# Attention buffers in another order, the cache loaded during layer 0's last expert, and five streams prepared ahead of the tokens' rows

## What is computed

```python
h = h + gmlp_mixer(rms_norm(h, norm_mix[0]), ...)
h = h + hier_moe(rms_norm(h, norm_ffn[0]), ...)          # 16 experts, 2 for each token
c = rms_norm(h, kv_norm) @ w_dkv                         # latent (256) and rotary key (32)
c_kv, k_rope = rms_norm(c[..., :256], ...), rope(rms_norm(c[..., 256:], ...), pos)
ckv_all = concatenate([past_ckv, c_kv]); krope_all = concatenate([past_krope, k_rope])
k_nope = rms_norm(einsum('blr,rhd->blhd', ckv_all, w_uk), k_nope_norm)   # per head
v = einsum('blr,rhd->blhd', ckv_all, w_uv)
q = low_rank_queries(rms_norm(h, norm_mix[1]))           # w_dq, norm, w_uq, norms, rope
o = softmax(masked(q_nope @ k_nope + q_rope @ k_rope) * SCALE) @ v
h = h + o @ w_o
h = h + hier_moe(rms_norm(h, norm_ffn[1]), ...)
```

## Time and profile before

| | |
|---|---|
| median of 3 runs | 1081.33 us |
| lowest and highest | 1079.39 and 1082.06 us |
| span of the profiled execution | 1080.6 us |
| granted clock of TensorE, mean over the span | 0.969 |
| PE busy (matmuls), DVE, ACT, POOL | 94%, 70%, 56%, 8% of the span |
| DMA | 278.95 MB, 258 GB/s in the mean |

### The profile page before, as it was taken

The page is one execution under the profiler, slowest core; times in us unless marked ns, Lnnn a source line. Parts: engine busy times, 40 slices in busy tenths (PEclk is TensorE's granted clock), DMA queues, the critical chain, the costliest instruction groups (busy, mean ns, idle before and its releaser), DMA issues.

```text
span 1080.6 us, 13540 instructions
## 1 busy us (share of the span) xinstructions
PE 1018.8 (94%) x5133; PEld 758.1 (70%) x5133; DVE 760.0 (70%) x645; ACT 605.0 (56%) x507; POOL 82.3 (8%) x109
## 2 busy tenths in 40 slices
PE   4999999999999999999969998989997989998997
PEld 4889998887666666666648686877785667766664
DVE  4456656267699888888815556662766999989896
ACT  5337432244577777777524233443536868887881
POOL 4000000004000000000021020000030000000003
PEclk9999999999999999999979999897898999999999
DMA  9542523684899999999366010303668999999984
GB/s 344 164 166 87 217 78 125 249 346 159 297 389 380 396 382 407 385 405 379 129 232 194 0 42 22 135 1 126 264 239 300 387 394 380 392 402 405 409 345 175
DMA packets 56923, 278.95 MB, mean 258 GB/s; under 512 B 6336, under 2 KB 10848, under 8 KB 48288
## 3 DMA queue, kind: packets, MB, share of 16 engines
q1 hardware_dynamic: 45424, 240.21, 57.7%
q0 software_dynamic: 8992, 29.74, 8.1%
q10 hardware_dynamic: 2464, 8.39, 2.0%
HBM read 260.45 MB, written 18.04 MB: 258 GB/s over the span
## 4 chain that ended last, share of the span: by engine, by line
PE 63%; issue 16%; DVE 8%; DMA 7%; ACT 3%; POOL 1%; ACTq 0%; SPq 0%; POOLq 0%; DVEq 0%
PE ps L189 19%; PE ps L195 9%; PE ps L527 4%; PE ps L581 4%; DMA raw<-in_moe_w_dram 4%; PE ps L624 3%; PE ps L1367 3%; PE ps L1364 3%; PE ps L2120 3%; PE ps L587 2%; PE ps L535 2%; DVE moe_wl L1104 2%; DVE raw_lo L1104 2%; PE ps L631 2%; PE ps L2095 1%
## 5 line engine op out<-in xcount | busy, mean ns | idle before, releaser
L1104 DVE TENSOR_TENSOR raw_lo<-raw,moe_wh 128x4096 fp32r<-128x4096 f32 x48 | 212.0, 4422 | 37.4 <-ACT moe_wh L1099 37.4
L1104 DVE TENSOR_TENSOR moe_wl<-moe_raw,moe_wh 128x4096 fp32r<-128x4096 f32 x48 | 212.0, 4422 | 33.6 <-ACT moe_wh L1099 33.4
L1099 ACT ACTIVATE moe_wh<-raw 128x4096 fp32r<-128x4096 f32 x48 | 174.0, 3625 | 20.8 <-DMA raw<-in_moe_w_dram 9.0
L1099 ACT ACTIVATE moe_wh<-moe_raw 128x4096 fp32r<-128x4096 f32 x48 | 173.9, 3624 | 14.1 <-DMA moe_raw<-in_moe_w_dram 14.1
L189 PE MATMUL ps<-moe_wh,moe_x 128*72 128x512 f32 x512 | 125.8, 398 | 1.7 <-DVE moe_x L1234 1.5
L189 PEld LDWEIGHTS ps<-moe_wh,moe_x 128*72 128x72 f32 x512 | 71.8, 143 | 46.0 <-DVE moe_x L1234 2.6
L329 DVE TENSOR_TENSOR raw_lo<-raw,gm_wh 128x4096 fp32r<-128x4096 f32 x12 | 53.1, 4424 | 69.6 <-ACT gm_wh L323 67.2
L189 PE MATMUL ps<-moe_wh,moe_hTh 128*72 128x512 f32 (+1 forms) x256 | 83.7, 410 | 4.9 <-DVE moe_hTl L1239 3.1
L189 PE MATMUL ps<-moe_wh,moe_hTl 128*72 128x512 f32 (+1 forms) x256 | 81.8, 401 | 0.0
L323 ACT ACTIVATE gm_wh<-raw 128x4096 fp32r<-128x4096 f32 x11 | 39.9, 3626 | 57.7 <-DMA raw<-in_gm_w_out_dram 29.2
L1364 PE MATMUL ps<-moe_wh,moe_x 128*128 128x512 f32 x224 | 58.9, 402 | 9.7 <-DVE moe_x L1234 9.7
(11 more groups left out here) (408 smaller groups left out, 1730.1 us busy)
## 6 DMA issues: line engine op xcount, KB each, us to landing
raw<-in_moe_w_dram SPq DMA_DIRECT2D x48, 2048.0 KB, 11.6
moe_raw<-in_moe_w_dram SPq DMA_DIRECT2D x48, 2048.0 KB, 11.9
raw<-in_gm_w_in_dram SPq DMA_DIRECT2D x7, 2048.0 KB, 7.9
raw<-in_gm_w_out_dram SPq DMA_DIRECT2D x4, 2048.0 KB, 7.6
moe_yrows<-moe_rows ACTq DMA_DIRECT2D x16, 288.0 KB
moe_rows<-moe_xrows POOLq DMA_DIRECT2D x14, 288.0 KB, 9.4
moe_rows<-moe_xrows POOLq DMA_DIRECT2D x14, 256.0 KB, 9.1
moe_yrows<-moe_rows ACTq DMA_DIRECT2D x14, 256.0 KB
```

The source lines that it names most:

```text
L1099: nc.scalar.activation(w_hi[hi][:], w_raw[slot], ACT.Copy).then_inc(wh_ready, 1)
L1104: nc.vector.tensor_tensor(w_lo[slot], w_raw[slot], w_hi[hi][:].bitcast(F32), ALU.subtract).then_inc(wl_ready, 1)
```

## The change

Four things are altered.

1. The attention's buffers are allocated in another order: `cTs`, `krT`, `psT`, `new_rinv`, `cTn` and `cqT` come first, on `moe_wh0` and `moe_wh1`, and `cst` and `w_uk` come to lie on the low parts of the weights 3 and 4, which are free at `w_used` = 45.
2. SP loads `w_uk` one product earlier (`3 * NE - 3`), and directly behind it both halves of the cache, before the overflow loop. `load_cache` is gone, and so is the second half's load in `at_sync`.
3. `turn_keys_up` stands before `product_y(15)` on TensorE, and `copy_keys_up` before `y_copy(15)` on ACT.
4. TensorE prepares stream 4 too before the rows, and then waits for `ch_c` 13 and `ch_sq` 10, since the rows' turns write the banks that ACT reads for that stream. Behind the projections come `prepare(5)` and `prepare(6)`, then `key_products(7)` between the first low-rank turn and the first query product; `turn_latent(0)` and `keys_and_values(0)` each come one place earlier. ACT's queue is reordered alike.

```diff
--- before.py
+++ after.py
@@ -833,8 +833,6 @@
                                      w_in_expert(l, name, e)).then_inc(s["w"], 16)
                     at_least(sp, s["act"], 5 * i + 5)
                     sp.dma_start(yrows[bass.ds(row, cap), :], rows[0:cap, 2, :]).then_inc(s["st"], 16)
-            if l == 0:
-                load_cache(sp)
             at_least(sp, s["st"], 16 * n_over + 16)
             sp.wait_ge(y_stored, 16 * (E0 + SENT if l else NE))
             sp.sem_inc(y_final, 1)
@@ -1205,10 +1203,10 @@
             experts(a, folding_step if l else step)
             if not l:
                 hidden_high(NE - 1)
+                copy_keys_up(a)
             y_copy(NE - 1, 1)
             if not l:
                 store_y(NE - 1, 1)
-                copy_keys_up(a)
             a.wait_ge(rt_table, l + 1)
             n_over = a.value_load(ovt_i[0:1, 2 * EXTRA:2 * EXTRA + 1], min_val=0, max_val=EXTRA)
             s = over[l]
@@ -1466,6 +1464,7 @@
             experts(pe, folding_step if l else step, {3: lambda: turn_kept(0)} if l else None)
             if not l:
                 transpose_hidden(NE - 1)
+                turn_keys_up(pe)
             if l:
                 pe.wait_ge(rt_hot, 4 + 1 + KEPT)
                 pe.wait_ge(y_out, E0 + NE - 1)
@@ -1483,8 +1482,6 @@
                         last = nc.tensor.matmul(ps[:, SPREAD[t][c]], kept_hot[0:cap, 1, t * P:(t + 1) * P].bitcast(F32),
                                                 rows[0:cap, 3, c * 512:c * 512 + 512], start=False, stop=True)
                     last.then_inc(spread, 1)
-            else:
-                turn_keys_up(pe)
             pe.wait_ge(rt_table, l + 1)
             n_over = pe.value_load(ovt_i[0:1, 2 * EXTRA:2 * EXTRA + 1], min_val=0, max_val=EXTRA)
             s = over[l]
@@ -1528,12 +1525,15 @@
         KC = 2 * P
         KALL = KC + DECS
         UNITS = [(0, 0, HEADS), (1, 0, HEADS // 2), (1, HEADS // 2, HEADS)]
+        cTs = sb("at_cache_cT", [P, DECB, 2, KC], F32, at)
+        krT = sb("at_krT", [QK, DECB + 1, KC], F32, at)
+        psT = sb("at_psT", [P, 2, 4 * P], F32, at)
+        new_rinv = sb("at_new_rinv", [P, P], F32, at)
+        cTn = sb("at_cTn", [P, 2, P], F32, at)
+        cqT = sb("at_cqT", [P, 3, P], F32, at)
         cst = sb("at_cache", [P, 2 * DECB, KVR + ROPE], F32, at)
-        cTs = sb("at_cache_cT", [P, DECB, 2, KC], F32, at)
         w_uk = sb("at_w_uk", [P, 2, HEADS * NOPE], F32, at)
-        krT = sb("at_krT", [QK, DECB + 1, KC], F32, at)
         rinv = sb("at_rinv", [P, DECB, KC], F32, at)
-        psT = sb("at_psT", [P, 2, 4 * P], F32, at)
         qa = sb("at_qa", [P, 2, DECB, HEADS * DECS], F32, at)
         sqT = qa[:].rearrange("p s b n -> p s (b n)")
         pcT = sb("at_pcT", [P, 2, HEADS, DECB, DECS], F32, at)
@@ -1552,7 +1552,6 @@
         ast = sb("at_stat", [P, 64], F32, at)
         qT = sb("at_qT", [QK, 2, HEADS, P], F32, at)
         qTs = gain2[0:QK].rearrange("p (b n) -> p b n", b=DECB)
-        cqT = sb("at_cqT", [P, 3, P], F32, at)
         turns = sb("at_turns", [P, 4, TILES, ROPE // 2], F32, at)
         kst = sb("at_kstat", [P, 2, HEADS], F32, at)
         kcat = sb("at_kcat", [P, 2, HEADS, QK], F32, at)
@@ -1560,8 +1559,6 @@
 
         kTp = raw[0:QK, 1, 0:HEADS * SEQ].rearrange("p (h k) -> p h k", h=HEADS)
         vp = raw[:, 1, HEADS * SEQ:HEADS * SEQ + 2 * HEADS * VD].rearrange("p (t n) -> p t n", t=2)
-        new_rinv = sb("at_new_rinv", [P, P], F32, at)
-        cTn = sb("at_cTn", [P, 2, P], F32, at)
         q_words = q_sb[:].rearrange("p t h n -> p (t h n)")
         s_sb = q_words[:, 0:DECB * KALL].rearrange("p (b k) -> p b k", b=DECB)
         sst = sb("at_sample_stat", [P, DECB, 3], F32, at)
@@ -1622,18 +1619,15 @@
                          ).then_inc(ld_cache[half], 16)
 
         def load_keys_up(sp):
-            sp.wait_ge(w_used, M_MOE[0] + 3 * NE - 2)
+            sp.wait_ge(w_used, M_MOE[0] + 3 * NE - 3)
             sp.dma_start(w_uk[:], A["w_uk"].rearrange("(k p) h n -> p k (h n)", p=P)).then_inc(ld_uk, 16)
-
-        def load_cache(sp):
-            sp.wait_ge(w_used, M_MOE[0] + 3 * NE - 1)
             load_cached(sp, 0)
+            load_cached(sp, 1)
 
         def at_sync(sp):
             sp.wait_ge(w_used, M_MOE[0] + 3 * NE)
             sp.dma_start(w_dkv, A["w_dkv"].rearrange("(k p) n -> p k n", p=P)).then_inc(ld_at, 16)
             sp.dma_start(w_dq, A["w_dq"][0].rearrange("(k p) n -> p k n", p=P)).then_inc(ld_at, 16)
-            load_cached(sp, 1)
             sp.dma_start(w_uq, A["w_uq"][0].rearrange("(k p) h n -> p k (h n)", p=P)).then_inc(ld_at2, 16)
             sp.dma_start(w_uv, A["w_uv"].rearrange("(k p) h n -> p k (h n)", p=P)).then_inc(ld_at2, 16)
             sp.wait_ge(at_qn, 1)
@@ -1903,6 +1897,7 @@
                 out = c_sb[:, t] if i == 0 else cq_sb[:, t]
                 nc.scalar.activation(out, ps[:, 4 + i, 0:KVR + ROPE if i == 0 else QR], ACT.Copy).then_inc(at_projc, 1)
 
+            squares(4)
             turned_rows(0, 0)
             turned_rows(0, 1)
             roots_of_keys(a, 0)
@@ -1923,19 +1918,18 @@
                 nc.scalar.activation(q_sb[:, t].rearrange("p (b h) n -> p b (h n)", b=2), ps[:, 4:6, 0:QR], ACT.Copy
                                      ).then_inc(at_qc, 1)
 
-            squares(4)
+            squares(5)
             root(a, ast[:, 0:9])
-            squares(5)
+            squares(6)
             low_queries(0)
-            squares(6)
+            squares(7)
             queries(0)
             low_queries(1)
-            squares(7)
+            latent_turned(a, 0)
             queries(1)
             low_queries(2)
-            latent_turned(a, 0)
+            values_and_squares(a, 0)
             queries(2)
-            values_and_squares(a, 0)
             latent_turned(a, 1)
             root(a, ast[:, 10:58])
             key_roots(a, 0)
@@ -2102,7 +2096,10 @@
             for b in range(4):
                 prepare(b, b % 2)
             sum_squares(3, 1)
+            prepare(4, 0)
             pe.wait_ge(ld_at, 32)
+            pe.wait_ge(ch_c, 13)
+            pe.wait_ge(ch_sq, 10)
             def turn_rows(t, i):
                 pe.wait_ge(at_xn, 2 * t + i + 1)
                 if t:
@@ -2185,18 +2182,17 @@
                     last = nc.tensor.transpose(ps[0:QK, 4 + hh // 4, (hh % 4) * P:(hh % 4 + 1) * P], kcat[:, n, hh], ident)
                 last.then_inc(at_KT, 1)
 
-            prepare(4, 0)
             prepare(5, 1)
+            prepare(6, 0)
             turn_low_queries(0)
-            prepare(6, 0)
+            key_products(7)
             query_products(0)
             turn_low_queries(1)
-            key_products(7)
+            turn_latent(0)
             query_products(1)
             turn_low_queries(2)
-            turn_latent(0)
+            keys_and_values(0)
             query_products(2)
-            keys_and_values(0)
             turn_latent(1)
             sum_squares(6, 0)
             keys_and_values(1)
```

## The result

| | before | changed |
|---|---|---|
| median | 1080.68 us (16 runs) | 1083.63 us (16 runs) |
| lowest and highest | 1076.69 and 1085.69 us | 1079.61 and 1087.38 us |
| ratio, with its 95% interval | | 1.0028 (1.0015 to 1.004) |
| span of the profiled execution | 1080.6 us | 1084.9 us |
| its time as a whole | not listed | 1086.6 us |

The account below looks back on a forecast made before the run. TensorE's waits between layer 0's last products and the attention's first queries were taken as the bound. Rows +5.1, projections -2.5, DVE's pauses -1.0 and -1.6 gave 0.0: 1080.6 plus 0.7 is 1081.3 us, range 1077.7 to 1084.6.

Parts of the forecast that it names:

- the hole: TensorE's idle 2.6 us before product_y(15); the moved turn_keys_up was to fill it, leaving 0.6 us.
- rival A: At product_y(15): the granted clock stays low despite the filled hole, so 1.5 us is not gained, 1083.2 us; chance 0.12.
- the 1.5 of the sum: product_y(15) ends 1.5 us sooner because the clock stays up behind the filled hole (bounds 0 and 1.6).
- the row that decided it: Clock window at the kernel's start, 13.3 to 16.8 us, read as transposes at 1.00, so transposes hold the clock.
- D: Behind the projections: DVE's pauses before tiny roots stay, up to +2.6 us, 1083.9 us; chance 0.09.
- step 1: Before the first turn_cache: empty overflow passes are a fixed 6.8 us from TensorE's arrival, so it starts 3.4 us sooner.
- step 2: The tokens' gathers keep their length, no gain taken, so the tokens' path and its root come 1.5 us sooner.
- the bound of 0.5 us on the other side: Gathers could land 0.5 us later because SP's queue is never paused by small packets.
- Rival C: At the gathers: rows land sooner without the cache in the queue, 1079.8 us, at most 1076.4; chance 0.15.
- step 3: Before key_products(3): TensorE waits 1.5 us for ACT, leaving 1.9 of the 3.4 us gain; a clock fall there was thought unlikely.
- rival B: The clock falls in TensorE's new pauses from key_products(3) to the rows, costing 1.6 to 4.0 us, 1082.9 to 1085.3; chance 0.12.
- step 4: Everything behind the queries' turn, layer 1 included, shifts with that moment, forecast at 0.0 us.

Follow-up runs that it names:

- e3: The changed kernel unaltered, run again for a second profile: ratio 1.0030 to before; 132.32 us from product_y(15) to the queries' turn.
- e14: The changed kernel unaltered, third profile: 132.42 us from product_y(15) to the queries' turn, 201.1 us to the samples' values product.
- e5: The kernel before with only the new buffer order and early loads; keys turned behind product_y(15), streams in old order: ratio 0.9983 to before.
- e9: The changed kernel with turn_keys_up and copy_keys_up behind product_y(15) again; early loads and five streams stay: ratio 1.0036 to before.
- e12: e5 with one pass of the overflow loop in layer 0 instead of 11: ratio 1.0043 to before.
- e1: The changed kernel with stream 4 prepared behind the projections again; early loads and early keys stay: ratio 1.0035 to before.
- e16: e1 unaltered, second profile: 131.16 us from product_y(15) to the queries' turn, 201.7 us to the samples' values product.
- e8: e2 with 16 needless matmuls (2.2 us) on TensorE right ahead of the queries' turn: ratio 0.9986 to before.
- e2: The changed kernel with ACT taking the root of the tokens' mean squares behind stream 2, not stream 1: ratio 1.0015 to before.
- e10: The changed kernel with 16 needless matmuls (2.2 us) on TensorE right ahead of the queries' turn: ratio 1.0030 to before.
- e6: e1 with 16 needless matmuls (2.2 us) on TensorE right ahead of the queries' turn: ratio 1.0021 to before.
- e11: The changed kernel with one pass of the overflow loop in layer 0 instead of 11: ratio 1.0024 to before.
- e13: The changed kernel with 14 needless matmuls (1.9 us) in TensorE's pause before key_products(3): ratio 1.0061 to before.

## Why the prediction was wrong

*Right.* The loads cost nothing. `turn_keys_up` fits in the hole, which shrank to 0.81 us (0.6 forecast), and rival A is out: the product ran at 1.00 and took 5.77 instead of 7.23 us from its start to its end, the 1.5 of the sum. In all eleven profiles of kernels with the keys turned ahead of it no low spell begins with the product; in the seven others one does, within 0.6 us of its start. What the Trainium skill says of transposes, weighed in the prediction ("TensorE: Matmul & The Clock Gate", "Part 4: PE-mode transpose"), does not hold here: 1.9 us of transposes and 0.8 us of idleness stood before the product, and the clock stayed up.

*Right by luck: the row that decided it.* The window from 13.3 to 16.8 us was read as transposes at the full clock. But the trace of before has no clock record ahead of 17.1 us, and these transposes ran at half speed: 16 of them take 3.67 us, 16 of the same form at 586.62 take 1.91.

```profile
12.87 3.67 PE L509 MATMUL ps<-const,gm_u 128*128 128x128 f32 x16 [0.89 <-DVE gm_u L180]
```

So that window says nothing of what transposes do to the clock; the changed kernel's own profiles do.

*Right again, in the middle.* The pause before the rows is 0.89 (0.85), that between the turns 1.09, the new one before the second query product 0.83 (1.0). DVE's two pauses are 0.31 and 0.28, so D is out. From the rows to the queries' turn the kernel takes 80.46 us in all three profiles, before 85.60: 5.1 less, as forecast (+5.1 to 0.0).

*Wrong, step 1: the 6.8 us pause as "a fixed length that begins when TensorE arrives".* The passes are the cause, as I said, but the sequencer goes through them beside the array. It begins when it has handed out the matmuls. In the sequencer's records of the changed kernel the loop's count is loaded at 543.17, 1.5 us into the product, and a pass follows every 0.73 us:

```
547.662 0.218 COMPARE_BRANCH 1488
547.938 0.029 MOVE           1488
548.026 0.214 COMPARE_BRANCH 1489
548.298 0.036 ALU_OP         1488
548.395 0.218 COMPARE_BRANCH 1488
```

(start us, us, instruction, line). Before, the queue ended with 16 transposes, which it had handed out by 549.54; from there the passes ran to 558.4, and only the 2.3 us up to the transposes' end were covered. Now 4.3 us of its 9.0 us lie beside the product, and the first turn comes 10.71 us behind the product's start, 5.0 sooner than before and not 3.4. The Trainium skill has the clue ("Advanced Engine Details and Errata", "Engine Queue Depths": 64 entries for TensorE). The trace agrees: the product with its weight loads is 48 instructions, and all were handed out 4.3 us before its end. The 1.6 us more were of no use: ACT's own passes, 0.44 us each, held its first copy to 555.35 (6.82 idle), and TensorE waited 2.47 us for it.

*Wrong, step 2: the gathers.* The root comes 33.91 us behind the product's start, 0.8 sooner than before and not 1.5 (34.21 and 34.31 in e3 and e14). y's copy and the first gather do come 1.5 sooner. From the first gather's issue to the root it is 23.7 us (575.61 - 551.93), before 23.0 (577.60 - 554.62); DVE waits 1.59 us for the third tile's rows, in e3 2.28, before 0.98. That is the bound of 0.5 us on the other side, and a bit more. Rival C, which got 0.15, was the wrong direction. It isn't that the cache left the queue: e5 and e9 have the same loads with the keys turned late and take 22.7 and 22.6 us, as the profiles of before do (22.7 to 23.0), while all eleven profiles with the early keys take 23.6 to 24.2. (e12, with late keys and one pass, takes 23.7.) What in them delays the rows stays open. With 0.15 more from the root to `key_products(3)` (1.86 where the sum had 1.7) it makes that product 1.05 sooner instead of 1.9, the rows +6.2 instead of +5.1, and the queries' turn +1.0 instead of 0.0.

*Wrong, step 3, the larger one: rival B got 0.12.* I took the pause before `key_products(3)` for 1.5 us. It was 2.13 to 2.87, since ACT's root comes 0.7 to 1.1 us later than I had it (TensorE's arrival is within 0.3 us of the forecast), and two of three profiles have the fall behind it, 2.0 us (132.3 and 132.4 against 130.3), within B's price of 1.6 to 4.0. It also takes back what the filled hole had given: low time in A is 13.7 us as before.

*Wrong, step 4: "all that follows hangs on that moment".* It does not: B is 66.8 to 73.3 us in eighteen profiles, with the same work, and follows its low time (66.8 to 68.0 at 13.7 us, 68.5 to 70.5 at 17.1, 73.1 to 73.3 at 23.9 to 25.4). The same kernel can differ by 2 to 4 us there (e1 and e16; the changed kernel's first profile and e3). That a shift at its start decides this is an inference that no run isolates. In the sum: +1.0 for the order, +2.0 in two of three for B's spell, which is 2.4 in the mean, and 0.7 in stretch B, which is within its scatter: 3.1 us, where the medians show 2.95. By the estimate above the same sum reads: the forecast's A had 1.5 us of work and waits more and 1.5 less for the clock; it got 2.9 more and only 0.4 less. Also mis-sized, and without weight for the difference: the time around the span is 1.7 us (1086.6 - 1084.9), not the 0.7 that I took from before's median and span. The times of the other kernels go the same way as A + B in the main. Exceptions are e8, which has 2.8 us more than before there and was not slower (its profiled execution took 1083.31 us, 2.0 above its median), and e2, with 4.0 us more there and 1.6 by its ratio (profiled 1085.08, 1.9 above its median).

What stays open is when a pause brings the clock down. Before `key_products(3)` none of 0.96, 2.13 and 2.26 us had a fall behind it, and all seven of 2.49 us and more had (e10, e14, e6, e3, e16, e12, e11). Yet pauses of 1.27 to 1.29 us ahead of the queries' turn had one in e13, e2 and e8 and none in the changed kernel.

## What to carry to other kernels

Cut a stage's gain into the work and the clock before you sum it: with the edits here, which shift a stage by 1 to 3 us, low spells came and went in it and behind it, and these are worth 1.7 us for each 3.4 us (an estimate: half of the low time). A pause that you make on TensorE has a price beyond its length, and filling it is no sure gain. Before a verdict on 0.3%, compare stretches over several profiles of either kernel: here A alone misled for e1, B alone for the changed kernel, and their sum came nearer to the times. And before a window's clock decides a term, hold the length of one instruction in it against the same form elsewhere.

## What the hardware showed

- An empty pass of the overflow loop costs 0.73 us on TensorE (two branches of 0.22 us), 0.44 on ACT and 0.63 on SP, in the records of their sequencers. On TensorE it runs beside the array's queued work: what follows such a loop is only late by what the queue doesn't cover.
- The granted clock is at 0.5 for 27 to 38 us of the 200 us from the last product to the values product, in every kernel here. Stretch B less half of its low time is 59.9 to 60.1 us in the four profiles with a filler ahead of it and 60.1 to 62.0 in the fourteen others.
- Needless matmuls of 2.2 us stood ahead of a stretch that was up to 4.3 us shorter (73.14 and 68.86, one profile each), and 1.9 us of them elsewhere went with a time some 3 us longer (1.0061 beside 1.0028 and 1.0030).
- The 16 transposes at 12.87 us ran at half the speed of the same form later (3.67 and 1.91 us), where the windows' view says 1.00; the trace's clock records begin at 17.1 us.
